# Low part of the gated product made by GpSimd instead of VectorE

## The reference, cut to what matters

```
def conv_ffn(h, rows, cols, w_up, conv_w, conv_b, w_down):
    u = (h @ w_up).reshape(bsz, rows, cols, 2 * D_FF)        # D_FF = 2816 = 22 x 128
    u = depthwise 3x3 convolution of u + conv_b
    a, v = jnp.split(u, 2, axis=-1)
    return (jax.nn.silu(a) * v).reshape(bsz, n, D_FF) @ w_down
```

## Time and profile before

| | us |
|---|---|
| median of 3 runs (3360.27 to 3363.6) | 3362.69 |
| the profiled execution's own time | 3364.44 |
| its span | 3362.6 |
| PE busy | 3128.3 (93%) |
| DVE busy | 1860.4 (55%) |
| ACT busy | 1146.1 (34%) |
| POOL busy | 912.9 (27%) |

### The profile page before, as it was taken

The page is one execution under the profiler, slowest core; times in us unless marked ns, Lnnn a source line. Parts: engine busy times, 40 slices in busy tenths (PEclk is TensorE's granted clock), DMA queues, the critical chain, the costliest instruction groups (busy, mean ns, idle before and its releaser), DMA issues.

```text
span 3362.6 us, 54509 instructions
## 1 busy us (share of the span) xinstructions
PE 3128.3 (93%) x22776; PEld 2952.1 (88%) x22776; DVE 1860.4 (55%) x3390; ACT 1146.1 (34%) x2097; POOL 912.9 (27%) x708
## 2 busy tenths in 40 slices
PE   6899999979999789999997999789999997999998
PEld 5699998969999779999996888679999995999997
DVE  1476374436666536727554454437737543784863
ACT  2333232234444323323223555423323223332322
POOL 0133323322322123233332112123332330333332
PEclk9999999989999799999998999899999998999999
DMA  8133333211111013333312111113333221222121
GB/s 342 72 138 127 135 122 132 72 57 54 51 54 57 30 51 128 134 131 128 101 62 67 48 48 48 46 51 135 127 138 117 96 71 62 66 75 77 54 74 62
DMA packets 95718, 305.78 MB, mean 91 GB/s; under 512 B 11248, under 2 KB 19696, under 8 KB 94832
## 3 DMA queue, kind: packets, MB, share of 16 engines
q1 hardware_dynamic: 85104, 286.71, 24.3%
q10 hardware_dynamic: 10368, 15.57, 1.3%
HBM read 297.52 MB, written 4.72 MB: 90 GB/s over the span
## 4 chain that ended last, share of the span: by engine, by line
PE 88%; DVE 8%; ACT 2%; issue 1%; DMA 1%; ACTq 0%; SPq 0%; DVEq 0%
PE acc L471 57%; PE acc L489 13%; PE acc L453 3%; PE acc L501 3%; PE acc L544 2%; PE acc L675 2%; PE acc L557 2%; PE acc L765 2%; PE acc L534 1%; DVE ffn_sq L1322 1%; DVE h_lo L1336 1%; DVE ffn_acc_v L1724 1%; DVE ffn_rstd L1310 1%; DVE ffn_acc_a L1724 1%; PE acc L597 1%
## 5 line engine op out<-in xcount | busy, mean ns | idle before, releaser
L445 POOL TENSOR_TENSOR w_lo<-w_raw,w_hi 128x512 fp32r<-128x512 f32 x704 | 912.7, 1318 | 2412.5 <-ACT w_hi L879 2412.4
L471 PE MATMUL acc<-h_hi,w_hi 128*128 128x320 f32 x2816 | 888.0, 315 | 39.7 <-DVE h_lo L1336 39.6
L471 PE MATMUL acc<-h_lo,w_hi 128*128 128x320 f32 x2816 | 874.9, 311 | 0.0
L471 PE MATMUL acc<-h_hi,w_lo 128*128 128x320 f32 x2816 | 874.7, 311 | 0.0
L879 ACT ACTIVATE w_hi<-w_raw 128x512 fp32r<-128x512 f32 x704 | 398.6, 611 | 724.6 <-DMA w_raw<-in_wall 394.2
L1724 DVE SCALAR_TENSOR_TENSOR ffn_acc_v<-acc,ffn_conv,ffn_acc_v 128x441 f32<-128x441 f32 (+3 forms) x880 | 544.3, 619 | 104.3 <-ACT ffn_acc_v L1247 104.3
L471 PEld LDWEIGHTS acc<-h_hi,w_hi 128*128 128x128 f32 x2816 | 532.9, 189 | 49.2 <-issue 35.0
L1724 DVE SCALAR_TENSOR_TENSOR ffn_acc_a<-acc,ffn_conv,ffn_acc_a 128x441 f32<-128x441 f32 (+3 forms) x880 | 545.2, 619 | 49.0 <-ACT ffn_acc_a L1247 39.5
L471 PE MATMUL acc<-g_hi,w_hi 128*128 128x320 f32 x1664 | 525.4, 316 | 18.1 <-DVE ffn_acc_a L1724 13.7
L471 PEld LDWEIGHTS acc<-h_lo,w_hi 128*128 128x128 f32 x2816 | 533.5, 189 | 0.0
L471 PEld LDWEIGHTS acc<-h_hi,w_lo 128*128 128x128 f32 x2816 | 532.9, 189 | 0.0
(11 more groups left out here) (174 smaller groups left out, 3300.1 us busy)
## 6 DMA issues: line engine op xcount, KB each, us to landing
w_raw<-in_wall SPq DMA_DIRECT2D x288, 512.0 KB, 4.0
mod_late<-in_wall SPq DMA_DIRECT2D x152, 512.0 KB, 3.3
mod_early<-in_wall SPq DMA_DIRECT2D x40, 512.0 KB, 8.7
w_raw<-in_wall SPq DMA_DIRECT2D x64, 256.0 KB, 2.9
w_raw<-in_wall SPq DMA_DIRECT2D x32, 384.0 KB, 3.0
box<-box_in ACTq DMA_DIRECT2D x2, 3008.0 KB, 16.0
x<-in_x SPq DMA_DIRECT2D x1, 2560.0 KB, 17.8
out_y<-pool_h SPq DMA_DIRECT2D x8, 320.0 KB, 3.0
```

What stands on the lines that cost most here:

```text
L445: nc.gpsimd.tensor_tensor(w_lo[j][:, cols], w_raw[j][:, cols], w_hi[j][:, cols].bitcast(F32), ALU.subtract).then_inc(lo_done, 1)
L471: mm = nc.tensor.matmul(result[j][:, c0:c1], w, h, start=(k == 0 and u == 0), stop=(k == nk - 1 and u == 2), skip_group_check=True)
```

## The change

DVE's `low_g` is taken away at both places, and the same subtraction is issued on GpSimd. It stands in GpSimd's list behind the low part of weight tile n+7, where n is the first job of the pair. Operands, widths and the semaphore that it raises stay.

```diff
+LOW_BEHIND = {n + 7: (PLAN[t][1], PLAN[t][2]) for n, t in enumerate(JOBS) if PLAN[t][0] == "up" and PLAN[t][2] < NPAIR}
...
         def _(pl):
+            def low_g(layer, p):
+
+                pl.wait_ge(g_rounded, NPAIR * layer + p + 1)
+                slot = p % RING_G
+                nc.gpsimd.tensor_tensor(g_lo[:, slot, :], sil[p % 2][:], g_hi[:, slot, :].bitcast(F32),
+                                        ALU.subtract).then_inc(g_ready, 1)
+
             for n in range(NJOBS):
...
                     nc.gpsimd.tensor_tensor(w_lo[j][:, cols], w_raw[j][:, cols], w_hi[j][:, cols].bitcast(F32),
                                             ALU.subtract).then_inc(lo_done, 1)
+                if n in LOW_BEHIND:
+                    low_g(*LOW_BEHIND[n])
...
-                        def low_g(d, side, slot):
-                            dve.wait_ge(g_rounded, d + 1)
-                            V.tensor_tensor(g_lo[:, slot, :], sil[side][:], g_hi[:, slot, :].bitcast(F32),
-                                            ALU.subtract).then_inc(g_ready, 1)
-
...
                                     if step == 4:
                                         gate(done - 1, 1 - pair, m)
-                                    if step == 7:
-                                        low_g(done - 1, 1 - pair, (p - 1) % RING_G)
...
                             gate(last, 1, n + 2 * count)
-                            low_g(last, 1, (p0 + count - 1) % RING_G)
```

## The result

The changed kernel takes 3349.31 us (median of 6 runs, 3347.91 to 3356.05) against 3362.66 us (6 runs, 3360.05 to 3366.8) for the kernel before in the same comparison: a ratio of 0.9963, 95% interval 0.9950 to 0.9976, or 13.35 us less. The forecast was 3356.9 us and its range ended at 3350.5. So the kernel is faster by more than the 6.7 us that can be told, by more than twice the 5.8 us of the sum, and the time lies outside the range. By the means of the same runs it is 12.3 us; the means are used from here on where small differences count.

A forecast was written before the change was run, and what follows sets the result against it. PE was taken to bound the kernel (busy 93%, 88% of the chain), DVE counting only at eight waits. The terms, -5.8 + 0 + 0 + 0 + 0 us against the median 3362.69, gave 3356.9 us; range 3350.5 to 3361.5.

The forecast's parts named there:

- Term 1: At eight MLP waits of PE (jobs 46 and 62), the last tap ends 0.73 us earlier without the low part: -5.8 us.
- Term 2: The other 80 of 88 low parts lie beside PE's jobs, where PE doesn't wait for DVE: zero.
- Term 3: POOL's new subtraction takes 1.65 us, 145 us more in all, covered by its idle time: zero, within 0 and +1 us.
- Term 4: Meetings where DVE's `low_g` and POOL's subtraction hold each other go away; neither is on the path: zero.
- Rival C: POOL's new operation holds a `gate` on the chain, up to 13.2 us less 5.8: slower, 3370.1 us; chance 0.04.
- Rival B: PE doesn't start earlier, as something else ends at the same time as the taps: 3362.7 us; chance 0.08.
- Rival A: The clock no longer falls at job 46 because the gap is shorter: 3348.7 us; chance 0.12.
- Term 5: The clock still falls after job 46's gaps, by luck after job 62's: zero, about 1.5 us either way.

The follow-up runs named there:

- h_twice: The kernel before, with the low parts of pairs 16 and 20 computed twice on DVE, the first into a spare buffer: 3370.01 us (1.0023).
- c_other80: Against the kernel before, 80 low parts go to POOL; the eight of pairs 16 and 20 stay on DVE: 3359.86 us (0.9991).
- c_again: c_other80 run once more, against the kernel before: 3363.87 us (0.9996).
- d_dve_late: The kernel before, with the low part kept on DVE but issued after the last tap of the pair, nothing on POOL: 3351.88 us (0.9975).
- a_again: The changed kernel run again with no edit, against the kernel before: 3352.70 us (0.9969).
- g: The kernel before, with filler matmuls at the end of job 45 and in job 46 ahead of the wait for `mod_s`: 3359.51 us (0.9983).
- j_pick_before: The kernel before, with job 46's product that waits for `mod_s` moved between the halves of its last block, layers 0 to 2: 3352.13 us (0.9965).
- l_fill62: The kernel before, with eight unused matmuls at the end of job 61, inside the 2.04 us wait of job 62: 3361.63 us (0.9993).
- b_only8: Against the kernel before, only the eight low parts of pairs 16 and 20 go to POOL; the others stay on DVE: 3355.52 us (0.9979).
- b_again: b_only8 run once more, against the kernel before: 3354.11 us (0.9972).
- f: The changed kernel, with filler matmuls at the end of job 45 and in job 46 ahead of the wait for `mod_s`: 3348.32 us (0.9956).
- m_third: The changed kernel run a third time with no edit, against the kernel before: 3349.99 us (0.9963).
- m_fourth: The changed kernel run a fourth time with no edit, against the kernel before: 3349.59 us (0.9964).

## Why the prediction was wrong

**Term 1 (the low part between the taps, -5.8 us): right.** 25.1 us became 19.2, 0.73 us at each of eight places, and the last tap stayed what PE waits for. h_twice gives the same 0.73 us with the other sign. The wait for `mod_s` was forecast at 2.5 us and is 2.08 to 2.5.

**Term 2 (the other 80 worth nothing): open.** c_other80 and c_again give 2.9 and 1.3 us by the means; both intervals reach 1, and both times the mean clock was a little higher than before.

**Term 3 (POOL, 1.65 us an operation, zero): right.** 1.575 us were measured, no wait in front of it or behind it. POOL's busy time grew by 119.8 us and not by 145, since the 88 take 138.6 us and the low parts of the weights 13.4 less than before. d_dve_late, with nothing on POOL, is 9.3 us below before, a_again 10.6 in the same comparison.

**Term 4 (fewer meetings, zero) and the rivals.** `w_lo` went from a mean of 1345 to 1324 ns and its longest from 2068 to 1882; nobody waited for it. Rival C is refuted: the gates stay at 818 ns. The rule of the Trainium skill (SBUF — State Buffer, section "Who interferes with whom") by which a gate would be held by POOL was given a chance of 4%. It holds in that POOL's instruction is held where the two meet (2.02 against 1.29 us in the earlier trace rows), but gates and POOL never meet here. That whoever comes first holds the other isn't shown: there POOL's instruction starts at 3166.56, 0.03 us ahead of DVE's, and it is the one that takes longer. Rival B is refuted by the waits. Rival A gave nearly the right time (3348.7) with the wrong mechanism: the clock still falls at job 46, in every profile of the changed kernel.

**Term 5 (the clock, zero) is the step that failed.** It had the mechanism and mis-sized it. The term was put at zero, with these words: "by luck of the moment", "may move the sum by about 1.5 us either way". The runs show about 1.8 us less at job 62 in its place, and not a gain or loss by chance. The places of 2.04 us had been called a matter of luck that stays; but the gap was to become 1.31 us, and what a shorter gap does to the odds wasn't asked. The runs give this table, from the rows of 408 matmuls in all profiles:

| wait at job 62 | clock fell | cost of one fall |
|---|---|---|
| 1.30 us (ten profiles) | 0 of 40 | |
| 2.04 us (before, c twice, g, j) | 6 of 20 | 1.5 us |
| 2.77 us (h_twice) | 4 of 4 | 1.3 to 2.8 us |

Each profile shows one execution, so the shares are rough. By them four gaps of 2.04 us cost 4 x 6/20 x 1.5 = 1.8 us on average (an estimate), and four of 1.30 us nothing; filling them in l_fill62 gave 2.4. That makes 5.8 + 1.8 = 7.6 us, and the upper group of the changed kernel is 7.9 us below before.

At job 46 the fall is still there and its price is less plain. In layers 0 to 2 the 24 matmuls took 17.4 us together before, and 16.4, 16.8, 16.4 and 16.7 in the four profiles of the changed kernel, some 0.8 us less. But c_again, with the old gaps, has 16.5, and b_only8, with the shorter ones, has 17.7, so these 0.8 us lie within the scatter of the profiles. In layer 3 the stretch from the first matmul of the first up job to the wait of job 62 went from 421.45 to 419.14 us. Of these 2.31 us, 0.73 is the wait of job 46, and only 0.33 are lost less at job 46 itself (its chain to job 62, before and after):

```profile
3184.68 80.26 PE acc L471 x528
...
3177.25 79.93 PE acc L483 x528
```

The other 1.25 us are in the first up job of the layer, where the clock of before falls once more (0.57 in 2866 to 2870) and that of after doesn't (1.00); 0.7 us of them are given back in the stage ahead. That leaves 0.9 us. With these the sum would be 9.3 us; b_only8 with b_again measured 8.4, d_dve_late 9.3. But the length of the gap doesn't explain the 0.9 us: j_pick_before has the old gap of 5.56 us in layer 3 and the stretch takes 419.42, h_twice has 6.30 us and it takes 419.91, and neither has the extra fall in the first up job. So these 1.7 us are seen, not explained.

**The rest goes along with the clock, and its cause is open.** 16 of 22 executions are another 6.1 us faster; between two profiles of the kinds 3.9 us are found in the mixer of layer 1, a stage that the change doesn't touch. A line through all runs puts 2.1 us of time to 0.001 of the mean granted clock; at an equal mean clock of 0.969 the changed kernel is 8.2 us below before, c is equal to before within 0.7 us, and b and d to the changed one within 1 us. What isn't settled is why the full change finds the better course so often (16 of 22) and b_only8 less (5 of 17 below 3352). The other 80 low parts may have a hand in it (term 2), but c_other80 had the short form of the mixer and c_again the long one. The moment at which the clock falls in the mixer goes with its length in all 17 profiles; it was not tested by itself.

**The range.** Its lower end was built from partial cases of rival A, and the scatter was taken from three runs (3.3 us). Six of the changed kernel span 8.1 us, and 90 of before 14.6. A range that adds 3 us on each side for this would have held the time, with the same wrong term in it.

## What to carry to other kernels

Where a chain of waits runs through one engine's list, look for instructions in it that nobody in the chain needs; where they go matters little, POOL and the end of DVE's own list gave nearly the same (10.6 and 9.3 us in one comparison). Then count PE's gaps by length: shortening those that lose the clock only sometimes gave, by the estimate above, another third of what the shorter waits gave. And a large wait that holds back work which doesn't need it, like the product waiting for `mod_s`, is best moved within the job: that gave 12 us for a few lines.

## What the runs showed of the hardware

- A gap of PE of 1.30 us never took the clock down (0 of 40), one of 2.04 us did in 6 of 20 and one of 2.77 us in 4 of 4, each behind matmuls at 1.00 (job 62, 16 profiles). With fillers in place of the gap it stayed at 1.00 (4 places at job 62 in l_fill62, 8 at job 46 in g and f).
- The same program takes different courses through a stretch with many short gaps: 47.3 us in the mixer of layer 1 where the clock falls twice (after), 43.3 and 43.4 where it falls once (a_again, m_third, m_fourth). The executions of the changed kernel lie in two groups 6.1 us apart, half of what the whole change gives.
- GpSimd's subtraction of 128x640 takes 1.575 us where VectorE's takes 0.82 to 0.83, below the 1.65 us that the two narrower widths gave.
